# Experts 4 to 15 loaded in the order of their token counts, and a first overflow round that reads weight slabs still in the ring

## What is computed

```python
def _hier_moe(h, w_rg, b_rg, w_re, b_re, w_gate, w_up, w_down):
    glog = (h @ w_rg + b_rg).astype(jnp.float32)
    gp, gi = lax.top_k(jax.nn.softmax(glog, axis=-1), 1)
    oh_g = jax.nn.one_hot(gi[..., 0], MOE_GROUPS, dtype=jnp.float32)
    elog = (jnp.einsum('bld,gde->blge', h, w_re) + b_re).astype(jnp.float32)
    elog_sel = jnp.einsum('blge,blg->ble', elog, oh_g)
    ev, ei = lax.top_k(elog_sel, TOP_K_E)
    ...
    a = jax.nn.silu(jnp.einsum('bld,gedf->blgef', h, w_gate)) * jnp.einsum('bld,gedf->blgef', h, w_up)
    return jnp.einsum('blgef,gefd->bld', a * combine[..., None], w_down)
...
        fp = _hier_moe(xp * (1.0 + mp[4]) + mp[3], *wm)
        xp = _layer_norm(ALPHA * xp + mp[5] * fp, ln_w[i, 1], ln_b[i, 1])
```

## Time and profile before

| | |
|---|---|
| median of 3 runs | 1422.3 us (1420.46 to 1427.87) |
| profiled execution, own time | 1427.28 us |
| its span | 1425.5 us |
| PE busy | 1279.0 us, 90% of the span |
| DVE, ACT, POOL busy | 513.9, 352.0, 158.9 us |
| DMA | 305.96 MB, mean 215 GB/s |
| chain that ended last | PE 72%, DMA 11%, DVE 8%, ACT 3%, issue 3%, POOL 2% |

### The profile page before, as it was taken

How to read it: one execution, slowest core, us unless ns; L and a number is a source line. 1 busy time by engine, 2 the same in 40 slices (tenths; PEclk the granted TensorE clock), 3 DMA queues, 4 the chain that set the end, 5 groups by cost and what they waited for, 6 DMA issues and landing times.

```text
span 1425.5 us, 15607 instructions
## 1 busy us (share of the span) xinstructions
PE 1279.0 (90%) x5924; PEld 691.1 (48%) x5924; DVE 513.9 (36%) x1189; ACT 352.0 (25%) x763; POOL 158.9 (11%) x222
## 2 busy tenths in 40 slices
PE   6999998999999999796769999899999999897944
PEld 3555555554565446342224565555556445543311
DVE  0343345442322024411104665547775022511105
ACT  1322331222300012211105322324546211211102
POOL 5000310000000000122003110012223000104001
PEclk9999997999999998798979999989999999599978
DMA  9566103337535442799988432443344195499984
GB/s 377 198 239 239 52 18 132 113 108 236 192 119 204 169 172 67 311 420 420 422 340 300 164 117 83 136 159 130 112 136 134 46 377 198 173 418 421 421 366 148
DMA packets 76214, 305.96 MB, mean 215 GB/s; under 512 B 7932, under 2 KB 16380, under 8 KB 59884
## 3 DMA queue, kind: packets, MB, share of 16 engines
q1 hardware_dynamic: 53984, 250.89, 46.5%
q10 hardware_dynamic: 17468, 37.67, 7.2%
q0 software_dynamic: 4688, 16.40, 3.1%
HBM read 278.08 MB, written 26.85 MB: 214 GB/s over the span
## 4 chain that ended last, share of the span: by engine, by line
PE 72%; DMA 11%; DVE 8%; ACT 3%; issue 3%; POOL 2%; SPq 0%; ACTq 0%; DVEq 0%; POOLq 0%
PE bank L530 20%; PE bank L552 12%; PE bank L676 5%; PE bank L891 4%; DMA arena<-in_moe_dn 4%; PE bank L1084 3%; PE bank L503 3%; DMA arena<-in_ln_rows 3%; DMA arena<-htok,tok_at 3%; PE bank L696 2%; DVE arena L2339 2%; PE bank L490 2%; PE bank L927 2%; PE bank L822 1%; PE bank L919 1%
## 5 line engine op out<-in xcount | busy, mean ns | idle before, releaser
L530 PE MATMUL bank<-hT,ring 128*128 128x384 f32 x896 | 299.6, 493 | 2.5 <-ACT hT L1423 1.7
L530 PEld LDWEIGHTS bank<-hT,ring 128*128 128x128 f32 x896 | 169.3, 192 | 121.7 <-issue 11.5
L552 PE MATMUL bank<-ring,arena 128*128 128x512 f32 (+1 forms) x512 | 173.4, 604 | 2.1 <-DVE arena L1995 2.1
L676 PE MATMUL bank<-arena,hT 128*64 128x512 f32 x448 | 111.9, 614 | 8.1 <-ACT hT L1556 6.1
L552 PEld LDWEIGHTS bank<-ring,arena 128*128 128x128 f32 (+1 forms) x512 | 72.4, 194 | 93.2 <-issue 86.6
L1829 DVE SCALAR_TENSOR_TENSOR arena<-arena,par 128x388 f32<-128x388 f32 x160 | 99.8, 624 | 5.6
L1084 PE MATMUL bank<-hT,ring 128*128 128x384 f32 x256 | 98.7, 509 | 0.0
L503 PE MATMUL bank<-ring,csil 128*32 128x256 f32 x768 | 68.3, 483 | 13.6 <-POOL ones L1281 6.7
L676 PEld LDWEIGHTS bank<-arena,hT 128*64 128x64 f32 x448 | 39.0, 141 | 69.5 <-issue 61.5
L1369 POOL TENSOR_TENSOR arena<-arena 128x192 f32<-128x192 f32 x64 | 40.6, 666 | 239.2 <-PE bank L1114 180.2
L2339 DVE TENSOR_SCALAR arena<-arena 128x128 f32<-128x128 f32 x192 | 52.1, 340 | 15.0 <-PE bank L1114 11.1
(11 more groups left out here) (376 smaller groups left out, 1607.7 us busy)
## 6 DMA issues: line engine op xcount, KB each, us to landing
arena<-in_moe_gu SPq DMA_DIRECT2D x72, 1024.0 KB, 17.7
ring<-in_ada_w SPq DMA_DIRECT2D x96, 512.0 KB, 5.0
arena<-in_moe_dn SPq DMA_DIRECT2D x30, 1024.0 KB, 24.3
ring<-in_b_w_in SPq DMA_DIRECT2D x40, 512.0 KB, 3.7
ring<-in_a_w_in SPq DMA_DIRECT2D x32, 512.0 KB, 3.6
arena<-acs_rows ACTq DMA_DIRECT2D x32, 384.0 KB, 3.6
ring<-in_moe_dn SPq DMA_DIRECT2D x10, 1024.0 KB, 25.5
yg<-arena ACTq DMA_DIRECT2D x18, 512.0 KB, 7.9
```

The source lines that it names most:

```text
L530: last = mm(keys[j][1][:, 0:T], w[:, k, P * j:P * j + P], hT[:, 4 * half + k, :], start=half == 0 and k == 0, stop=half == 1 and k == 3, s ...
L552: last = mm(keys[t][1][p:p + tokens.shape[1], :], tokens, w[:, j, :], start=k == 0, stop=k == KE - 1, skip_group_check=True)
L676: last = mm(ps[CAP * u:CAP * u + CAP, :], m_hg[:, q % 2, P * k + CAP * u:P * k + CAP * u + CAP], w[u][:, j, :], start=k == 0, stop=k == KD ...
```

## The change

- **Order.** Experts 0 to 3 (FIXED) stay in places 0 to 3. Experts 4 to 15 take places 4 to 15 by their token counts, the heaviest last: DVE ranks them by comparing keys (count x 1024 + 64 x expert), permutes the 0/1 matrices accordingly, and writes the order into `plan`. SP waits for it before slab 10, reads nine places into registers, and loads every later slab from a computed address.
- **Slabs.** The fixed list has 39 slabs. The last 12 loads of the pairs' order are in the loop: gate/up of places 13, 14, 15, down of 13, 14, 15, and gate/up and down of place 16, which is the expert of place 15 once more. They land while pairs 6 and 7 are worked and pairs 6 and 7 read them.
- **First round.** It loads nothing of its own: its four seats are places 15, 16, 14 and 13, whose slabs are still in the ring. The plan takes two chunks of the heaviest and one each of the next two (m_held) out of the rest, and quads becomes 1 + ceil(rest / 4). Slots are marked free by held_used when the round has read them; SP waits for that before the next ln_rows and the next ada_w slabs.
- **Moved.** The plan's remaining DVE work goes from before pair 0 to behind it. tok2 goes from after pair 1 to after pair 3, ln_rows from before slab 26 to before slab 34, and new_x is done one tile at a time before the gathers of pairs 5, 6 and 7. Slabs 10 and 11 are not fetched ahead any more. m_sel2 is one matrix instead of two. Two more fills of yg at the start; some semaphores are merged.

```diff
+        add_expert("gu", (0, 1))
+        for q in range(1, 6):
+            add_expert("gu", (2 * q, 2 * q + 1))
+            add_expert("dn", (2 * q - 2, 2 * q - 1))
+        add_expert("gu", (12,))
+        add_expert("dn", (10, 11))
+        add_expert("dn", (12,))
+        assert len(order) == MSLABS
+        add_expert("gu", (13,))
+        add_expert("gu", (14, 15))
+        add_expert("dn", (13, 14, 15))
+        add_expert("gu", (16,))
+        add_expert("dn", (16,))
+        SEATS = (15, 16, 14, 13)
```

On TensorE, the place of tok2, and the waits of the round for slabs that are loaded during the pairs:

```diff
-                    if q == 1:
+                    if q == 3:
                         pe.wait_ge(sem("sel_ready"), (2 * NT + 1) * (l + 1))
...
+                    for j in (0, 1, 3):
+                        pe.wait_ge(sem(f"ow_in{j}" + L), p * loop_in[j] + loop_in[j])
```

On SP, the order read from the plan, the place of ln_rows, and the wait behind the loop:

```diff
-                for m in range(12, MSLABS):
-                    if m == 26:
+                sp.wait_ge(sem("planned"), 2 * l + 1)
+                for place in range(FIXED, 13):
+                    o = ORDER + place - FIXED
+                    at_place[place] = sp.value_load(plan[0:1, o:o + 1], min_val=0, max_val=NEXP - 1)
+                for m in range(10, MSLABS):
+                    if m == 34:
                         sp.wait_ge(filled, group["tok2", l][1])
                         norm_rows(2 * l)
                     weights(l, m)
...
+                sp.wait_ge(sem("held_used" + L), quads * OVER + OVER)
```

On POOL, the norm by tiles:

```diff
-                    if q == 5:
-                        new_x(2 * l, range(NT))
+                    if q >= 5:
+                        new_x(2 * l, (q - 5,))
```

On DVE, the sort, the order, the chunks that the first round takes, and the number of rounds:

```diff
+                link(ve.scalar_tensor_tensor(out=m_key, in0=m_cnt[:, FIXED:], scalar=1024.0, in1=m_e64[:, FIXED:],
+                                             op0=ALU.mult, op1=ALU.add))
+                link(ve.tensor_tensor(out=m_q, in0=m_key.unsqueeze(1).to_broadcast([P, FREE, FREE]), in1=bc(m_key, FREE),
+                                      op=ALU.is_le))
+                link(ve.tensor_reduce(m_rank, m_q, X, ALU.add))
...
+                ve.tensor_scalar(plan[0:1, ORDER:ORDER + FREE], m_top[0:1, :], 1.0 / CAP, None,
+                                 ALU.mult).then_inc(sem("planned"), 1)
...
+                link(ve.tensor_tensor(out=m_n, in0=m_n, in1=m_held, op=ALU.subtract))
+                link(ve.tensor_scalar(m_n, m_n, 0.0, None, ALU.max))
...
+                ve.tensor_scalar(plan[0:1, QUADS:QUADS + 1], m_quad[:, 0:1], 1.0, None, ALU.add).then_inc(sem("planned"), 1)
```

More of the change, by code:

```diff
@@ L671, in gate_up @@
                     for half in (0, 1):
[L672 removed]
+                        w = landed_slabs("gu", (2 * q, 2 * q + 1), half)
                         for j in range(4):
@@ new lines, in moe @@
+                listed(0, 0, 2)
+                for t in range(NT):
+                    ins = ve.tensor_tensor(out=m_tmp[:, t], in0=m_q,
+                                           in1=m_p1[:, t, FIXED:].unsqueeze(1).to_broadcast([P, FREE, FREE]), op=ALU.mult)
+                link(ins)
+                link(ve.tensor_reduce(m_pp, m_tmp, X, ALU.add))
+                select(FIXED, NEXP, m_pp, (0,))
+                link(ve.tensor_tensor(out=m_tmp[0:1, 0], in0=m_q[0:1],
+                                      in1=m_e64[0:1, FIXED:].unsqueeze(1).to_broadcast([1, FREE, FREE]), op=ALU.mult))
```

352 lines of the change are left out of this document (202 added, 150 removed).

## The result

| | before | changed |
|---|---|---|
| median of the runs, us | 1423.03 (1420.46 to 1427.87, 4 runs) | 1448.12 (1445.45 to 1448.65, 4 runs) |
| profiled execution: span, us | 1425.5 | 1445.9 |
| mean granted clock | 0.932 | 0.921 |
| bytes moved by DMA | 305.96 MB | 288.15 MB |

The change makes the kernel slower: ratio 1.0169, 95% interval [1.0138, 1.0199]. The forecast was 1428 us (range 1402 to 1442), so it was wrong, by 20 us, and the range did not reach either.

A forecast was written before the change was run, and what follows sets the result against it. Saturated DMA, with waits for ln_rows and the loop's weights, was taken to bound the expert stages. Layer 0's +7.8 and layer 1's -2.1 gave +5.7 on 1427.28, so 1433.0; less 5.0 to the median, 1428 us (range 1402 to 1442).

The forecast's parts named there:

- Small items at nothing: Outside the stages: two more yg fills at 320 us and other small items cost nothing, covered by TensorE's own work.
- Rows outside these two stages are left alone: Outside the expert stages (575 to 765 and 1227 to 1425 us), the change does nothing apart from small items.
- From the trace to the median, -5.0 us: End of the sum: profiled execution stood 5.0 us above the runs' median of 1422.3, so 1433.0 became 1428.
- One round in each layer, 102 slabs: Loop of each expert stage: one round before and after, with 102 expert slab loads where there were 120.
- The sort and the register loads: Before slab 10: first plan write at 578.3, slab 10 at 583; nothing charged, 0 to 7.5 us in the range.
- the rival with them: Register loads starve the queue before slab 10: everything behind 7.5 us later in both layers, 1443 us; chance 0.23.
- The plan block hidden: Behind pair 0: pairs up to 5 are 11 us later, free on the path because pair 5 waits longer.
- ln_rows in front of pair 5: Before pair 5: ln_rows goes out later and lands at 659, so pair 5's tokens come +15.0 us, layer 1 +14.1.
- The loop without its wait: After the last down projection: no wait for weights, 17.8 us to the write; -16.7 us, in layer 1 -17.5.
- What waits for the held slabs: After layer 0's loop: ln_rows and ada_w wait until the round is read, gate rows +9.5 us; layer 1 +1.3.
- The sum of the stages: Both expert stages: layer 0 +7.8 us, layer 1 -2.1 us, together +5.7 us.
- the bytes win: Rival in the expert stages: ln_rows does not delay pair 5, last weights bound the stage; 1401 us, chance 0.22.

The follow-up runs named there:

- experiment 3: Changed kernel with POOL's gathers of all pairs ahead of new_x and VectorE's second plan block behind tokens(1): 1429.96 us, ratio 1.0019.
- 12: Changed kernel with gathers ahead of new_x, plan block behind tokens(1) and the yg fills at 146 us: 1425.47 us, ratio 0.9983.
- experiment 6: Changed kernel with each of SP's nine register loads right before the first slab that needs it: 1447.08 us, ratio 1.0128.
- experiment 2: Changed kernel with VectorE's second plan block moved from ahead of acts(0) to behind tokens(1): 1439.13 us, ratio 1.0088.
- experiment 1: Changed kernel with POOL's new_x tiles of both layers behind the gathers of all eight pairs: 1442.55 us, ratio 1.0089.
- experiment 8: Changed kernel with TensorE's three ada units of layer 0 behind the mix instead of ahead of the gate rows: 1447.23 us, ratio 1.0129.
- experiment 9: Changed kernel with layer 0's second ln_rows load behind the six ada_w slabs and the gathers: 1443.35 us, ratio 1.0107.
- five edits: Changed kernel with gathers ahead of new_x, plan block behind tokens(1), fills at 146 us, register loads one by one, ln_rows behind ada_w and gathers: 1419.35 and 1419.86 us.
- experiment 15: Kernel before with gathers ahead of new_x, its four yg fills at 146 us, and layer 0's ln_rows behind ada_w and gathers: 1425.80 us, ratio 0.9982.
- experiment 4: Changed kernel with the six yg fills issued at about 146 us instead of 323 us: 1443.74 us, ratio 1.0099.
- experiment 10: Kernel before with POOL's new_x behind the gathers of all pairs: 1429.17 us, ratio 1.0006.
- 7: Changed kernel with down slabs of places 13 to 15 held outside ring and the next ln_rows behind the six ada_w slabs: 1459.51 us, ratio 1.0232.
- 11: Changed kernel with gathers ahead of new_x, plan block behind tokens(1), fills at 146 us, and down slabs of places 13 to 15 outside ring: 1437.51 us, ratio 1.0048.
- 13: Changed kernel with five edits, first measurement: 1419.35 us, ratio 0.9923.
- 14: Changed kernel with five edits once more, with more rounds: 1419.86 us, ratio 0.9937.

## Why the prediction was wrong, step by step

- **"Small items at nothing: two more yg fills ... Their cover is TensorE's own work there": this step failed.** The fills cost 5.0 us in the traces (the stretch of VectorE, 24.9 for 19.9 us), 3 to 4 by medians. The cover that was named was TensorE's work, but the fills do not compete with TensorE; they compete with out_C's stores, on which ScalarE, and behind it TensorE, waits. The windows of the kernel before have a DMA share of 1.13 from 325 to 330 us and 0.99 to 335: the engines were already full there, and the prediction did not reckon with it.
- **"Rows outside these two stages are left alone": failed with it.** 11 of the 15 us by which the traces miss the forecast sum (+20.4 against +5.7) lie outside the stages. Apart from the fills' 5 they are 2 us ahead of 340 us and 4.3 between the stages, and these follow where the half clock falls. Between the mix of layer 0 and the routing of layer 1 the changed kernel has 30.7 us at half clock and the kernel before 20.5. The work there is the same, and kernels 3 and 12 of the table, whose programs are the changed kernel's in that stretch, have 20.5 us at half clock and take 491 us. I did not find what decides it, nor whether the change has a part in it; that stays open.
- **From the trace to the median, -5.0 us: failed.** The other 5 us of the 20 are this step. The traced execution of the kernel before stood 5.0 above a median of three executions, and I took this off. The changed kernel's stood 0.5 below its median, and the kernel before has medians of 1428.0 to 1428.7 us beside the experiments, so its trace was an ordinary one and the median of three was low. Whether by chance or by the chip is not shown.
- **One round in each layer, 102 slabs:** right.
- **The sort and the register loads:** right, with every size. The first plan write was put at 578.3 and slab 10 at 583; less the 6.8 us of late start they are at 577.5 and 582.9. The nine loads took from 584.3 to 589.7, 0.6 us each. The Trainium skill (DMA: Bandwidth & Descriptors, Latency and other measured facts) gives about 600 ns as the floor of a tensor_load, and the trace agrees. That they cost nothing in the changed kernel is shown by experiment 6; the rival with them falls.
- **The plan block hidden:** right as the sum used it (experiment 2: 2.0 and -0.2 us), and right in size: pair 0's acts are 9.7 us later in the stage, and pair 1's matmuls take 9.50 us instead of 7.1. But "if that cover were gone it would be 11 us in each layer" was too much: 7.5 and 2.7 (experiment 3 less 1).
- **ln_rows in front of pair 5:** the mechanism was right, the size too small in layer 0. ln_rows left at 649.4 (in the clock of the kernel before; forecast about 648), but landed at 662.9 instead of 659, so pair 5 is 18.7 us later instead of 15.0; in layer 1 15.8 instead of 14.1, within the bounds of +9 and +21.
- **The loop without its wait:** right. From the end of the last down projection to the write it is 17.7 us (728.84 to 746.52; forecast 17.8), at full clock.
- **What waits for the held slabs:** +7.6 us (write to gate rows 17.0, before 9.4), forecast +9.5. It has two halves. The write takes 9.0 us instead of 5.0 until ScalarE's mark, beside the burst; the gate rows then follow it by 8.0 us instead of 4.2, for ada_w. The second half goes when the ada units are moved (experiment 8: gate rows 0.8 us behind the mark), and comes back behind the mix. Whether the first half goes down with less in the burst is not settled (experiment 9). In layer 1 the mix is 2.2 us later behind the write instead of 1.3.
- **The sum of the stages:** +7.8 and -2.1 forecast, +8.8 and +0.2 measured. The rival "the bytes win" was described rightly as what happens once ln_rows is not in front of pair 5, but its price was not: with the gathers ahead alone (experiment 1) the stage of layer 0 is still 169.9 us.

**Where the 22.4 us of bytes went.** By the windows they became idle time of the DMA engines: the hole at 620, and the 24 us from 721 to 745 in which TensorE does pair 7 and the loop one after the other and SP may load nothing, since all seats are held. With five edits the byte-bound stretch ends at 702, and the same serial tail stands behind it. In layer 1, where no ada_w waits for the seats, 6 to 8 us of the 22.4 are left as gain (152.5 against 160.2 of experiment 15 and 158.5 of the other three traces of the kernel before); in layer 0 only 1.0 (159.1 against 160.1), which is within what two traces differ by. That ada_w and the slower write eat the rest there is argued from their 7.6 us above; no run took both away.

## What to carry to other kernels

Before a transfer is costed at nothing, name what shares the DMA engines with it at that time, and who waits for that; here 1 MB more, 260 us ahead of the expert stage, cost 3 to 5 us, where the whole forecast sum was 5.7. When bytes are cut from a stage whose DMA is full, look for what runs behind the last byte: slabs held for reuse keep the queue from being filled, so the saving turns into idle DMA unless the next loads have seats. Take the step from a trace to a median from many executions: three were 5 us off here. And try edits against two waits in one stage together as well as singly: the single ones gave 5.0 us in layer 0, the two together 10.5.

## What the runs showed that I had not expected

- A stop of TensorE of 1.7 us at 342 us was followed by a half clock from 345 to 352; with the stop gone (experiment 4), the clock stayed full there. Kernel 2, which has the six fills at their old place, shows only 3.4 us at half clock there, and the kernel of experiment 10, with four fills and a stop of 0.19 us ahead of the same matmuls, shows 3.4 us too: the same stop does not always cost the same.
- Executions of one program differ by up to 14 us (the kernel before: 1419.9 to 1434.2 us on one chip), and the mean granted clock goes with it (0.934 at the fastest, 0.925 at the slowest). In a stretch in which the program was not touched, two traces differ by 4 us. A single trace of 1430 us can therefore not price an edit of 4 us by its span. A stage's length in one trace is no better where the half clock falls otherwise: layer 1's stage took 158.7 us in the changed kernel and 159.5, 159.7 and 163.7 in experiments 8, 9 and 4, whose edits stand outside it. Differences of 1 to 2 us between stages in the tables above can therefore not be called effects.
- The last store of yg, 0.5 MB, took 4.5 to 5.0 us to ScalarE's mark in layer 0 in the four traces of the kernel before and its edits, and 7.5 to 9.9 us in all thirteen of the changed kernel and its edits. With ln_rows alone issued beside it, it took 7.9 and 7.7 us (experiments 7 and 11), with ada_w alone 7.5 to 9.0 (9, 13 and 14), and with both 8.2 to 9.9. In layer 1, where no ada_w stands, it took 2.9 to 3.2 us in the kernels before and 5.4 to 7.5 beside ln_rows. So either load slows it, and what each adds beside the other cannot be read from these traces.
